# Modulation rows of a diffusion block: sums over partitions by split fp32r products in place of fp32

## The reference

```python
mod_lat = silu(c) @ w_ada + b_ada                      # 6 x 1024
sh1, sc1, g1, sh2, sc2, g2 = split(mod_lat, 6)
x = x + g1 * (gated_merge(...) @ w_o)                  # first gated residual
h = rmsnorm(x, norm2_g) * (1 + sc2) + sh2              # second norm, modulated
x = x + g2 * conv_ffn(h)                               # second gated residual
out = rmsnorm(x, final_g)
```

## Time and profile before

| | us |
|---|---|
| median of 3 runs | 853.37 (852.27 to 854.98) |
| the profiled execution | 852.57 |
| its span, first to last instruction | 850.8 |
| around the span | 1.8 |
| TensorE busy | 808.2 (95%) |
| VectorE busy | 471.8 (55%) |
| GpSimd busy | 376.0 (44%) |
| ScalarE busy | 373.9 (44%) |

### The profile page before, as it was taken

How to read it: one execution, slowest core, us unless ns; L and a number is a source line. 1 busy time by engine, 2 the same in 40 slices (tenths; PEclk the granted TensorE clock), 3 DMA queues, 4 the chain that set the end, 5 groups by cost and what they waited for, 6 DMA issues and landing times.

```text
span 850.8 us, 11214 instructions
## 1 busy us (share of the span) xinstructions
PE 808.2 (95%) x3900; PEld 672.6 (79%) x3900; DVE 471.8 (55%) x600; ACT 373.9 (44%) x571; POOL 376.0 (44%) x191
## 2 busy tenths in 40 slices
PE   6779978999999999999999989999999999999996
PEld 4458856888888888888788978888888888888884
DVE  5854698788887467788413646555555555100005
ACT  7763365656565442232234644444444444211124
POOL 0086274345533455455455034444444444444434
PEclk9979999999999999999999989999999999999998
DMA  9822211111111488777355014333333332323312
GB/s 317 289 74 61 64 50 50 50 50 29 48 50 26 153 252 259 252 247 219 127 198 148 2 50 123 99 99 99 99 99 98 92 96 93 96 95 98 99 50 99
DMA packets 119134, 97.79 MB, mean 115 GB/s; under 512 B 13532, under 2 KB 100857, under 8 KB 119097
## 3 DMA queue, kind: packets, MB, share of 16 engines
q1 hardware_dynamic: 119065, 97.28, 37.1%
q10 hardware_dynamic: 32, 0.01, 0.0%
HBM read 95.17 MB, written 2.10 MB: 114 GB/s over the span
## 4 chain that ended last, share of the span: by engine, by line
PE 59%; issue 16%; POOL 9%; DVE 6%; DMA 4%; ACT 2%; SPq 2%; POOLq 0%; DVEq 0%; ACTq 0%
PE ps L374 16%; PE ps L375 15%; PE ps L376 15%; POOL wlo L318 8%; PE ps L1444 7%; PE ps L1426 3%; PE ps L1415 2%; DMA raw<-w_in_dram 2%; DMA raw<-w_o_dram 1%; POOL ht L525 1%; DMA xt<-ctx_dram 1%; DMA xt<-x_dram 1%; DVE wlo L318 1%; DVE work L1022 1%; SPq L425 1%
## 5 line engine op out<-in xcount | busy, mean ns | idle before, releaser
L318 POOL TENSOR_TENSOR wlo<-raw,whi 128x1024 fp32r<-128x1024 f32 (+4 forms) x126 | 287.8, 2292 | 423.8 <-ACT whi L310 401.6
L374 PE MATMUL ps<-hhi,whi 128*128 128x512 f32 (+1 forms) x560 | 214.7, 383 | 8.8 <-DVE hlo L962 5.3
L375 PE MATMUL ps<-hlo,whi 128*128 128x512 f32 (+1 forms) x560 | 213.5, 381 | 0.0
L376 PE MATMUL ps<-hhi,wlo 128*128 128x512 f32 (+1 forms) x560 | 213.2, 381 | 0.0
L310 ACT ACTIVATE whi<-raw 128x1024 fp32r<-128x1024 f32 (+3 forms) x127 | 123.3, 980 | 141.1 <-PE ps L376 77.8
L374 PEld LDWEIGHTS ps<-hhi,whi 128*128 128x128 f32 x560 | 106.8, 191 | 30.1 <-issue 6.4
L376 PEld LDWEIGHTS ps<-hhi,wlo 128*128 128x128 f32 x560 | 106.7, 191 | 20.0
L375 PEld LDWEIGHTS ps<-hlo,whi 128*128 128x128 f32 x560 | 106.8, 191 | 19.6 <-issue 0.2
L1208 DVE SCALAR_TENSOR_TENSOR work<-ps,prm,work 128x511 f32<-128x511 f32 x44 | 33.0, 750 | 82.0 <-ACT work L875 81.1
L1113 DVE SCALAR_TENSOR_TENSOR adacc<-ada,cvec,adacc 128x1024 f32<-128x1024 f32 x28 | 64.9, 2357 | 14.8 <-DMA ada<-w_ada_dram 14.8
L875 ACT ACTIVATE work<-ps,prm 128x512 f32<-128x512 f32 x44 | 34.2, 778 | 79.2 <-PE ps L376 79.2
(11 more groups left out here) (245 smaller groups left out, 1430.1 us busy)
## 6 DMA issues: line engine op xcount, KB each, us to landing
raw<-w_up_dram SPq DMA_DIRECT2D x88, 256.0 KB, 3.1
raw<-w_in_dram SPq DMA_DIRECT2D x66, 256.0 KB, 3.4
ada<-w_ada_dram SPq DMA_DIRECT2D x32, 512.0 KB, 6.1
raw<-w_down_dram SPq DMA_DIRECT2D x44, 256.0 KB, 2.7
adaraw<-w_ada_dram SPq DMA_DIRECT2D x32, 256.0 KB, 4.8
raw<-w_o_dram SPq DMA_DIRECT2D x16, 256.0 KB, 3.0
xt<-x_dram SPq DMA_DIRECT2D x4, 512.0 KB, 6.4
raw<-w_attn_out_dram SPq DMA_DIRECT2D x8, 256.0 KB, 2.9
```

What stands on the lines that cost most here:

```text
L318: ins = (engine or nc.gpsimd).tensor_tensor(out=l, in0=r, in1=h.bitcast(F32), op=ALU.subtract)
L374: pe.matmul(o, l[0], r[0], start=start, stop=False)
L375: pe.matmul(o, l[0], r[1], start=False, stop=False)
L376: return pe.matmul(o, l[1], r[0], start=False, stop=stop)
```

## The change

ACT makes an fp32r copy of `ones` before the merge loop (`onesr`). In d = 7, ahead of its sigmoids, ACT copies `adacc` in four pieces of 1024 columns to an fp32r high part `adahi`; DVE, also at the head of its d = 7, subtracts in four pieces to get the low part `adalo`. TensorE's `gate_rows` then waits for all four low parts, and makes four pairs of fp32r matmuls (high, then low, accumulated) in place of four fp32 ones. The column sums become 16 pairs of fp32r matmuls with two columns of `onesr` (two equal result columns, of which one is read) in place of 16 fp32 ones. The other lines of the diff place the new tensors in SBUF.

```diff
+            nc.scalar.activation(onesr[:], ones[:], ACT.Copy).then_inc(s("onesr"), 1)
+
             for d in range(DT):
                 b, w = 4 * (d % 2), 3 * (d % 2)
+                if d == DT - 1:
+                    for g in range(4):
+                        act.wait_ge(s("ada2_used"), 4 * DT - 3 + g)
+                        nc.scalar.activation(adahi[:, g * D:(g + 1) * D], adacc[:, g * D:(g + 1) * D], ACT.Copy).then_inc(s("ada_hi"), 1)
                 for n in range(3):
...
                 if d == DT - 1:
+                    for g in range(4):
+                        dve.wait_ge(s("ada_hi"), g + 1)
+                        nc.vector.tensor_tensor(out=adalo[:, g * D:(g + 1) * D], in0=adacc[:, g * D:(g + 1) * D],
+                                                in1=adahi[:, g * D:(g + 1) * D].bitcast(F32), op=ALU.subtract).then_inc(s("ada_lo"), 1)
                     gate_rows()
...
-            nc.vector.tensor_tensor(out=mod[:, 3 * DT:5 * DT], in0=ps[:, 0, 0:2 * DT], in1=prm[:, R_BADA + 3 * DT:R_BADA + 5 * DT],
+            nc.vector.tensor_tensor(out=mod[:, 3 * DT:5 * DT], in0=ps[:, 0, 0:4 * DT].rearrange("p (m s) -> p m s", s=2)[:, :, 0], in1=prm[:, R_BADA + 3 * DT:R_BADA + 5 * DT],
...
-                pe.wait_ge(s("ada2_used"), 4 * DT)
+                pe.wait_ge(s("onesr"), 1)
+                pe.wait_ge(s("ada_lo"), 4)
                 pe.wait_ge(s("m_prod"), 2 * DT - 2)
                 for n, at in enumerate((0, 512, 3 * D, 3 * D + 512)):
-                    pe.matmul(ps[:, n, :], ones[:], adacc[:, at:at + 512], start=True, stop=True).then_inc(s("gbc_ps"), 1)
+                    pe.matmul(ps[:, n, :], onesr[:], adahi[:, at:at + 512], start=True, stop=False)
+                    pe.matmul(ps[:, n, :], onesr[:], adalo[:, at:at + 512], start=False, stop=True).then_inc(s("gbc_ps"), 1)
...
             pe.wait_ge(s("gbc_sum"), 1)
             for m in range(2 * DT):
-                last = pe.matmul(ps[:, 0, m:m + 1], adacc[:, D + m * P:D + (m + 1) * P], ones[:, 0:1], start=True, stop=True)
+                pe.matmul(ps[:, 0, 2 * m:2 * m + 2], adahi[:, D + m * P:D + (m + 1) * P], onesr[:, 0:2], start=True, stop=False)
+                last = pe.matmul(ps[:, 0, 2 * m:2 * m + 2], adalo[:, D + m * P:D + (m + 1) * P], onesr[:, 0:2], start=False, stop=True)
             last.then_inc(s("cols2_ps"), 1)
```

More of the change, by code:

```diff
@@ L110, in build @@
         ones = sb("ones", [P, P])
+        onesr = sb("onesr", [P, P], F32R)
         eps = sb("eps", [P, 1])
@@ L159, in build @@
         sb("gap1", [P, 2 * HEADS * T], scope=mrg)
-        sb("gap4", [P, 2 * CT * T], scope=mrg)
+        adahi = sb("adahi", [P, 4 * D], F32R, scope=mrg)
         mhi = sb("mhi", [P, DT, T], F32R, scope=mrg)
@@ L167, in build @@
         mrg.close()
+        mods = ExitStack()
+        sb("gap5", [P, 2 * HEADS * T + 4 * D + 2 * DT * T + 3 * D + 512], scope=mods)
+        adalo = sb("adalo", [P, 4 * D], F32R, scope=mods)
+        mods.close()
         out_w = ExitStack()
```

## The result

The changed kernel takes 861.35 us (median of 6 runs, 857.96 to 863.97), the kernel before 853.35 us (6 runs). The ratio is 1.0083, 95% interval 1.0056 to 1.0111, so 4.8 to 9.5 us slower. The forecast was 861.5 us.

The account below looks back on a forecast made before the run. TensorE was taken to bound the kernel from the merge on. Stall 7.4, gate sums -1.6, clock 2.4 and column sums 0 gave +8.2 us: 860.8, or 861.5 us on the median's footing, range 857.0 to 864.5.

Parts of the forecast that it names:

- Bound: From the merge to the end, a microsecond added to or taken from TensorE's stream changes the time by a microsecond.
- The gate sums: TensorE's `gate_rows`: 8 fp32r matmuls take 1.8 us in place of 3.43, a gain of 1.6 us.
- rival 4: In `gate_rows`, fp32r matmuls with `onesr` cost two passes, 6.9 us in place of 1.8: 866.6 us; 0.03 with others.
- The chain to the fourth low part: ACT copies, then DVE subtractions alternating with POOL's; the fourth ends at 420.7 us, TensorE's first matmul follows at 420.9.
- Rival 1: POOL does not cut in before DVE's fourth subtraction: stall 5.1 us, time 858.5 to 859.3 us; chance 0.17.
- The hole: TensorE, ready for `gate_rows` at 413.54 us, stalls until 420.9 for the low parts: 7.4 us.
- The clock: After the stall before `gate_rows` TensorE runs at half clock for 3.3 to 6.2 us, costing 1.6 to 3.1, middle 2.4.
- The column sums: After the merge, 32 weight loads still set the pace at 0.112 us each: no difference, bounds +0.3 to -1.8 us.
- Rival 2: Column sums' fp32r loads go twice as densely and the clock does not fall after them: +4.8, 858.2 us; chance 0.11.
- The sum: Whole kernel: 7.4 - 1.6 + 2.4 + 0 = +8.2 us against 852.57, so 860.8, or 861.5 us on the median's footing.
- Rival 3: No stall before `gate_rows`, splits done when TensorE comes; only the 1.6 us gain stays, 851.8 us; chance 0.07.

Follow-up runs that it names:

- the filled version: Changed kernel with 24 further matmuls, their results overwritten, run on TensorE before it waits for the low parts: 859.44 us, ratio 1.0065 to the kernel before.
- the version with GpSimd held: Changed kernel, but ACT splits unit 1 of the output projection only after all four low parts: 858.9 us, ratio 1.0074 to the kernel before.
- the repeat: The changed kernel itself, unaltered, run once more beside the kernel before on the same chip: 861.28 us, ratio 1.0091; its profiled execution took 862.23 us.

## Why the prediction was right, point by point

- **Bound.** That a microsecond in TensorE's stream after the merge is one in the time fits the loss: 8.0 us measured, 6 to 7.3 us by the terms below. It does not hold for gains: the versions with interleaved column sums and with the column sums first took time out and got stalls at the second norm's transposes. The prediction's sentence "and the same for one taken away" was wrong there. The forecast did not need it, except for the 1.6 us.
- **The gate sums.** 1.6 us expected. At full clock they take 1.8 us (8 times 0.23 in the filled version), as worked out, and with that rival 4 (two passes with `onesr`) is out. In the changed kernel they run at half clock and take 3.4 us, which the prediction had under its clock term.
- **The chain to the fourth low part.** From the start of `mlo`'s subtraction to the fourth low part it gave 10.2 us (410.53 to 420.7); measured 10.06 (410.02 to 420.08). Each turn is there: first subtraction held by GpSimd until 413.4, the fourth 3.36 us long, GpSimd's next started at 416.24 inside the third. Rival 1 is out by these rows, and the version with GpSimd held shortened just the fourth.
- **The hole.** 7.4 us expected, idle times of 5.5, 5.6, 6.0 and 6.4 us in four profiles that have the full wait. The step that was mis-sized is the start of the wait, not its end. I took TensorE's arrival (413.54) and VectorE's state (410.53) from one execution. They are 3.0 us apart there, 4.4 and 4.5 us in the two profiles of the changed kernel, 3.3 in the filled one. VectorE comes to d = 7 after adds that wait for DMAs and for turns with GpSimd, TensorE does not; that this makes the difference vary is argued, not shown.
- **The clock.** 2.4 us expected, in a range of 1.6 to 3.1. The slow stretch about the hole's end is 3.4 us in one profile and 6.8 in others. Half of what lies behind the restart is 1.6 us in the first profile (420.2 to 423.4) and 2.9 us in the repeat (421.7 to 427.4). Filling the hole gave back 1.5 to 2.2 us. On the chip where both were compared, the median clock of the changed kernel is 0.0065 under that of before, which would be up to 5.6 us, but the mean counts idle time too, where a low clock costs nothing.
- **The column sums.** 0 expected; 0.11 us a load in both. Rival 2 with its dense fp32r loads is out: 192 ns a load, no gain, and the clock fell behind the sums as before. The rule of the Trainium skill weighed there (TensorE: Matmul & The Clock Gate, "Weight-path perf modes": fast loads for types other than FP32) doesn't apply to fp32r in these traces.
- **The sum.** 7.4 - 1.6 + 2.4 = 8.2 against a measured 8.0 (4.8 to 9.5). With the measured terms it is 6.0 - 1.6 + 1.6 to 2.9 = 6.0 to 7.3. So the agreement within 0.2 us is partly luck: the hole was taken 1.4 us too long, and 0.7 to 2 us of the measured loss belong to no term. They are within the interval. A candidate is the slow stretch behind the column sums, 3.4 us before and in the first profile but 6.8 us in the repeat; no run was made to show it. The sign, the mechanism and the order of the terms are what the runs bear out.
- **Rival 3** (not slower) would have needed the splits out of TensorE's way. The two versions with the gate sums after the branch outputs come near that case: ratio 0.9993 with 1.9 us of wait left, and 0.9966 and 0.9984 with only the gate vectors split.

## What to carry to other kernels

A cheaper instruction pays only if its operands are ready when the dear one's were. Here 1.6 us of products were bought with eight instructions on two other engines, placed by program order at the very moment of use; the same products 5.4 us later in TensorE's stream, and only for the half that profits, made the kernel 1.4 to 2.9 us faster. Look as well at what a block of cheap-looking work covers (here VectorE's products) before it is moved, and at a second chain that runs beside: in three versions here TensorE waited 1.9 to 3.8 us where the two meet, and the chain shows in no wait of the kernel before between 405 and 485 us. When a wait is costed from one profile, take the distance between the two engines' arrivals from several repetitions, for it varied here by 1.5 us.

## What the runs showed of the hardware

- A subtraction with two SBUF operands on VectorE, 1.21 us alone, took 3.36 us when GpSimd's was ready during the one ahead of it, and the two engines took turns though VectorE's next subtraction was ready too. I had expected this from the earlier trace rows. It came out so in all four profiles with the full wait: 8.15 us for the four subtractions each time.
- A matmul of one or two columns costs 0.11 us in a block and 0.117 us between matmuls of 512 columns; there its weight loads did not hide beside them.
- The clock fell within or behind 3.6 us of such tiny matmuls though TensorE counted as busy all the while, in every profile where they stand in one block but that of the version with GpSimd held. Between 300 and 840 us the slow stretches lasted 3.4 or 6.8 us in all the profiles, and nothing between. Which of the two comes is not decided by the kernel alone: after the hole it differed between two executions of the changed kernel. How much of the spread this makes differs: the correlation of time and mean clock is -0.93 and -0.81 for the changed kernel, and -0.40 and -0.66 for the two sets of the version with only the gate vectors split.
